# The opening of a two-layer trunk: the norm row cleared and spread by products over 128 partitions, the first half slab's split on VectorE and GpSimd, idle transposes first

## The reference

```
h = rms_norm(x, norm_mix_pre[i])                 # x * rsqrt(mean(x*x) + eps) * w
mix = ssd_mixer(h, ...)  if i == 0 else pool_mixer(h, ...)
x = x + rms_norm(mix, norm_mix_post[i])
f = conv_ffn(rms_norm(x, norm_ffn_pre[i]), ...)
x = x + rms_norm(f, norm_ffn_post[i])
```

## Time and profile before

| | us |
|---|---|
| median of 3 runs | 1150.98 |
| the profiled execution | 1151.16 |
| its span, first to last instruction | 1149.4 |
| TensorE busy | 1141.1 |
| VectorE busy | 684.4 |
| ScalarE busy | 523.9 |
| GpSimd busy | 32.8 |

### The profile page before, as it was taken

How to read it: one execution, slowest core, us unless ns; L and a number is a source line. 1 busy time by engine, 2 the same in 40 slices (tenths; PEclk the granted TensorE clock), 3 DMA queues, 4 the chain that set the end, 5 groups by cost and what they waited for, 6 DMA issues and landing times.

```text
span 1149.4 us, 14668 instructions
## 1 busy us (share of the span) xinstructions
PE 1141.1 (99%) x5734; PEld 956.9 (83%) x5734; DVE 684.4 (60%) x783; ACT 523.9 (46%) x614; POOL 32.8 (3%) x87
## 2 busy tenths in 40 slices
PE   9999999999999999999999999999999999999998
PEld 8888888888788898888888888899888888888886
DVE  5678778888943865565555412487655565562124
ACT  5667676767523644444344211465444344342213
POOL 6000001000000000000000000000000000000000
PEclk9999999999999999999999999999999999999999
DMA  8243444443222323332322332512222323323321
GB/s 271 75 130 129 128 129 129 128 129 129 74 94 90 110 75 117 102 104 80 108 94 88 110 110 92 183 37 74 92 90 93 109 79 103 109 76 111 106 74 74
DMA packets 85246, 121.74 MB, mean 106 GB/s; under 512 B 4167, under 2 KB 71215, under 8 KB 85200
## 3 DMA queue, kind: packets, MB, share of 16 engines
q1 hardware_dynamic: 85018, 121.02, 32.1%
q10 hardware_dynamic: 182, 0.07, 0.0%
HBM read 118.92 MB, written 2.16 MB: 105 GB/s over the span
## 4 chain that ended last, share of the span: by engine, by line
PE 97%; DVE 2%; ACT 0%; issue 0%; POOL 0%; DVEq 0%; POOLq 0%; ACTq 0%
PE bank L994 28%; PE bank L300 18%; PE bank L302 18%; PE bank L301 18%; PE bank L497 6%; PE bank L777 2%; PE bank L786 1%; PE bank L414 1%; PE bank L709 1%; PE bank L736 1%; PE bank L1170 0%; DVE w_lo L270 0%; PE bank L764 0%; PE bank L437 0%; PE bank L432 0%; PE bank L1185 0%
## 5 line engine op out<-in xcount | busy, mean ns | idle before, releaser
L300 PE MATMUL bank<-h_hi,w_hi 128*128 128x512 f32 x928 | 364.1, 392 | 0.0
L302 PE MATMUL bank<-h_hi,w_lo 128*128 128x512 f32 x928 | 361.3, 389 | 0.0
L301 PE MATMUL bank<-h_lo,w_hi 128*128 128x512 f32 x928 | 361.1, 389 | 0.0
L270 DVE TENSOR_TENSOR w_lo<-raw,w_hi 128x2048 fp32r<-128x2048 f32 x90 | 206.2, 2291 | 219.7 <-ACT w_hi L265 219.7
L516 DVE SCALAR_TENSOR_TENSOR tmp<-bank,par,tmp 128x511 f32<-128x511 f32 (+2 forms) x248 | 184.7, 747 | 135.3 <-ACT tmp L507 122.4
L265 ACT ACTIVATE w_hi<-raw 128x2048 fp32r<-128x2048 f32 x90 | 171.5, 1906 | 152.5 <-PE bank L994 152.3
L302 PEld LDWEIGHTS bank<-h_hi,w_lo 128*128 128x128 f32 x928 | 174.2, 188 | 36.6
L301 PEld LDWEIGHTS bank<-h_lo,w_hi 128*128 128x128 f32 x928 | 174.3, 188 | 36.3 <-issue 0.7
L300 PEld LDWEIGHTS bank<-h_hi,w_hi 128*128 128x128 f32 x928 | 174.2, 188 | 36.4 <-issue 0.7
L507 ACT ACTIVATE tmp<-bank,par 128x512 f32<-128x512 f32 x112 | 86.3, 775 | 229.4 <-PE bank L302 209.5
L994 PE MATMUL bank<-w_hi,act_hi 128*128 128x512 f32 x348 | 107.2, 389 | 0.0
(11 more groups left out here) (193 smaller groups left out, 1035.9 us busy)
## 6 DMA issues: line engine op xcount, KB each, us to landing
raw<-in_ffn_w_up SPq DMA_DIRECT2D x44, 1024.0 KB, 5.1
raw<-in_ffn_w_down SPq DMA_DIRECT2D x22, 1024.0 KB, 5.0
raw<-in_ssd_w_in SPq DMA_DIRECT2D x19, 1024.0 KB, 5.5
decay<-ac_dram SPq DMA_DIRECT2D x16, 512.0 KB, 4.3
raw<-in_ssd_w_out SPq DMA_DIRECT2D x8, 1024.0 KB, 4.9
from_start<-ac_dram SPq DMA_DIRECT2D x32, 128.0 KB, 4.0
xres<-in_x SPq DMA_DIRECT2D x4, 512.0 KB, 5.7
result<-xres SPq DMA_DIRECT2D x3, 512.0 KB, 2.6
```

The costliest lines, as they stand in the source:

```text
L270: dve.tensor_tensor(lo[:], raw[n % 2][:], hi[:].bitcast(F32), ALU.subtract).then_inc(lo_ready, 1)
L300: pe.matmul(dst, wh, xh, start=first, stop=False, **kw)
L301: pe.matmul(dst, wh, xl, start=False, stop=False, **kw)
L302: return pe.matmul(dst, wl, xh, start=False, stop=last, **kw)
```

## The change

VectorE first clears all 128 partitions of `pre_b` (new semaphore `pre_clear`), and ScalarE's queue waits for that before it loads the norm row into partition 0. The spread then multiplies the whole 128x128 tile of ones with all 128 partitions of `pre_b`, of which 127 are zero. The high part of the first half slab moves from ScalarE to VectorE, behind the scaling of chunk 1; its low part moves from VectorE to GpSimd, ahead of the window matrices. TensorE starts with nine idle transposes once the identity is there, then waits for the other constants and the norm row; five follow the spread. One parameter piece of 4 KB moves from ScalarE's queue to SP's.

```diff
-        def first_part_hi(act):
-            act.wait_ge(part_in, 16)
-            act.activation(w_hi[0][:, FIRST_PART], raw[0][:, FIRST_PART], ACT.Copy).then_inc(part_hi, 1)
+        def first_part_hi(dve):
+            dve.wait_ge(part_in, 16)
+            dve.tensor_copy(w_hi[0][:, FIRST_PART], raw[0][:, FIRST_PART]).then_inc(part_hi, 1)
...
-        def first_part_lo(dve):
-            dve.wait_ge(part_hi, 1)
-            dve.tensor_tensor(w_lo[0][:, FIRST_PART], raw[0][:, FIRST_PART], w_hi[0][:, FIRST_PART].bitcast(F32),
+        def first_part_lo(pool):
+            pool.wait_ge(part_hi, 1)
+            pool.tensor_tensor(w_lo[0][:, FIRST_PART], raw[0][:, FIRST_PART], w_hi[0][:, FIRST_PART].bitcast(F32),
                               ALU.subtract).then_inc(part_lo, 1)
...
-                pe.matmul(bank[:, PRE_BANK + j, :], ones[0:1, :], pre_b[0:1, j * T:(j + 1) * T], start=True,
+                pe.matmul(bank[:, PRE_BANK + j, :], ones[:], pre_b[:, j * T:(j + 1) * T], start=True,
                           stop=True).then_inc(pre_spread, 1)
...
             first_load(sp, w_in_slabs[Z_SLABS + X_SLABS])
-            load_params(sp, par_pieces[4:])
+            load_params(sp, par_pieces[3:])
...
             pool.wait_ge(consts, 4)
+            first_part_lo(pool)
...
         def _(pe):
+            pe.wait_ge(consts, 3)
+            keep_busy_pe(pe, 9)
             pe.wait_ge(consts, 4)
-            keep_busy_pe(pe, 4)
             spread_pre_pe(pe)
-            keep_busy_pe(pe, 4)
+            keep_busy_pe(pe, 5)
...
         def _(act):
+            act.wait_ge(pre_clear, 1)
             act.dma_start(pre_b[0:1, :], norm_mix_pre[0:1, :]).then_inc(pre_in, 16)
-            load_params(act, par_pieces[:4])
+            load_params(act, par_pieces[:3])
             act.wait_ge(consts, 4)
             root_table_act(act)
             x_stats_act(act, 0, 0)
             x_stats_act(act, 0, 1)
-            first_part_hi(act)
...
         def _(dve):
+            dve.memset(pre_b[:, :], 0.0).then_inc(pre_clear, 1)
             prime(dve, "vector")
...
             scale_dve(dve, 0, 1, pre_view(), (pre_spread, 2))
+            first_part_hi(dve)
             last_part_hi(dve)
             features_dve(dve, 0, 0)
             features_dve(dve, 0, 1)
-            first_part_lo(dve)
             last_part_lo(dve)
```

More of the change, by code:

```diff
@@ L195, in hybrid_trunk @@
         x_sq, x_rms, x_rr, xn_ready = sem("x_sq"), sem("x_rms"), sem("x_rr"), sem("xn_ready")
-        pre_spread, pre_kept, xn_half = sem("pre_spread"), sem("pre_kept"), sem("xn_half")
+        pre_clear, pre_spread, pre_kept, xn_half = sem("pre_clear"), sem("pre_spread"), sem("pre_kept"), sem("xn_half")
         tr_done, h_hi_ready, h_ready = sem("tr_done"), sem("h_hi_ready"), sem("h_ready")
```

## The result

The changed kernel takes 1152.88 us (median of 16 runs, 1152.09 to 1153.75) against 1150.72 us before (16 runs, 1149.89 to 1151.81): ratio 1.0019, 95% interval 1.0012 to 1.0025. It is 2.2 us slower where 1.4 us less was forecast, and outside the range.

What follows compares the result with a forecast made beforehand. TensorE, busy 1141.1 of 1149.4 us, was taken as the bound; pass 2 ending at 15.1 instead of 16.49 saves 1.4 us, giving 1149.6 against the median of 1150.98. Range 1148.8 to 1151.5 us.

Steps and rivals of the forecast that it cites:

- Clearing and the norm row: Opening: memset takes 0.69 us, the row's DMA is issued at about 1.55 and lands at 4.09, upper bound 5.75.
- The spread: Norm row's products on TensorE: lower level for all but the last piece, over at 7.6 us (bounds 5.9 and 7.87).
- The wait that I priced at 0.37 us: TensorE's new idling for the norm row, after nine idle transposes end at 3.72 us.
- VectorE, ScalarE's queue: Opening: table load at 3.3, first reciprocal at 6.44, chunk 1 scaled by 9.86, casts by 11.1, fourth h_lo at 13.65.
- TensorE: Opening: chunk 1's transposes start at 9.9, block products at 11.2, pass 2 ends at 15.1 against 16.49: 1.4 us less.
- GpSimd's low part: First half slab's subtraction: 2.4 us after the second cast at 11.1, done at 13.5, at worst 14.05, hidden.
- (b): Rival: GpSimd gets the port pair before VectorE's second cast; pass 2 ends at 17.45, 1.0 slower, 1152.0 us; chance 0.09.
- (d): Rival: norm row lands at 5.75, spread ends at 9.53, pass 2 at 16.6, 1151.1 us; chance 0.07.
- (c): Rival: TensorE's gaps keep the level low through pass 1; pass 2 ends at 17.8, 1.3 slower, 1152.3 us; chance 0.06.
- (a): Rival: the level rises no earlier than before, near 12.5; pass 2 ends at 16.6, 1151.1 us; chance 0.16.
- The base: Profile of the kernel before: pass 2 ends at 16.49 us, span 1149.4, execution 0.18 above the median of 1150.98.

Runs made afterwards that it cites:

- the second profile: The changed kernel run again without an edit, against the kernel before; its profile ended pass 2 at 18.47 us, against 17.35 in the first.
- row_ahead: Changed kernel with the norm row's DMA at the head of SP's queue, behind the clearing and ahead of all loads: 1150.93 us (one run).
- spread_only: Kernel before with only the clearing, the wait for it and the 128-row spread added: 1152.99 us.
- gap_filled: Changed kernel with 20 idle transposes ahead of the spread instead of nine: median 1150.81 us, against 1150.87 before.
- row96: Changed kernel with the norm row on partition 96, partitions 0 to 95 cleared beside the load, and a 97-row spread: median 1149.87 us.
- row96_only: Kernel before with only the norm row on partition 96, its clearing and the 97-row spread: 1149.55 us, ratio 0.9990.
- row96_split_back: row96 with the half slab split as in the kernel before (high part on ScalarE, low part on VectorE): median 1149.91 us.
- row96_early: row96_only with six idle transposes from the identity on instead of four from the triangle on: 1149.61 us, ratio 0.9989.
- before_again: The kernel before run again without an edit, for its profile: pass 2 ended at 15.80 us, not 16.49.
- split_only: Kernel before with only the moved split (first half's high part on VectorE, low part on GpSimd): 1150.88 against 1150.87 us.
- one_row: Changed kernel without the clearing and with the one-row spread of before: 1.5 us faster than the changed kernel, 0.8 above before.

## Why the prediction was wrong, point by point

**Clearing and the norm row: wrong, and the first step that failed.** I had it issued at 1.55 and landed at 4.09. VectorE began at 1.10 and not at the other engines' 0.81, the memset took 0.92 and not 0.69, so the issue was at 2.04; the flight took 3.70 to 4.87 us in four profiles, not 2.54. The landing at 5.74 is near the upper bound of this very step (5.75, the 4.2 us of a transfer issued into traffic), but by luck: 1.55 + 4.2 there, 2.04 + 3.70 here, and the second profile has 6.91. I had that row and took the other, because it was the same transfer. But in the rows before it was issued together with the first x chunk, and the change put it behind both x chunks; row_ahead shows that without loads ahead of it (and on SP's queue) it lands in 1.73 us at most, clearing and all.

**The spread: wrong, and the second step.** I let the level rise during it. It rose at 10.8, behind it (at about 10.5, at its very end, in the second profile). The wait that I priced at 0.37 us was 1.91 (3.07 in the second profile), and with it nine idle transposes were worth nothing: the kernel with the old four and the late row, spread_only, takes the same time. That this, and not the lateness alone, is the larger part, gap_filled shows: with the row later still (6.27), the medians differ by 2.2 us. The early row has a further part: row96 is 0.75 below its before, gap_filled 0.06.

**VectorE, ScalarE's queue: right in kind.** First root used at 6.82 (6.44 forecast), the table load at 3.93 (3.3 forecast, at most 3.85); the gap between last scaling and h_lo is as worked out (casts of 0.68 and 0.69, h_lo in 2.47). All of it stood 2 us later, behind the spread. The moved parameter piece did nothing visible.

**TensorE: the structure right, the start wrong.** From chunk 1's scaling on, the steps were 1.09, 0.44 and 3.96 us. They began at 11.86 instead of 9.9.

**GpSimd's low part: right, with a risk wrongly weighed.** 2.71 us with the cast ahead of it (2.4 forecast), over by 15.3 and hidden. The port's order (b) went as I said in the changed kernel's profile, and against VectorE in row96's, where its data came late.

**The rivals.** (d), the row at 5.75, is what happened, with 0.07 for its chance. Its spread end (9.53, measured 9.65) and its last h_lo (15.6, measured 15.4) were right; its price of 0.1 us was not, for pass 2 ended 0.86 us later than before. I let h_lo decide, and had left out that transposes, idle transposes and 32 products follow chunk 1's scaling one by one: 11.86 + 1.09 + 0.44 + 3.96 = 17.35. (c), a gap that keeps the level down, was at work at the same time. I had priced and weighed the two as alternatives though the late row makes the gap. (a) falls with gap_filled and row96: idle transposes and wide, mostly zero rows both raise the level.

**The base.** The profile of before was a late draw of its own opening (16.49, again 15.80). Of the 2.2 us between the medians the two first profiles show 0.86 at the end of pass 2; the second pair shows 18.47 - 15.80 = 2.67. The typical difference lies between. What sets the point of the rise from run to run stays open.

## What to carry to other kernels

- A preparation that a DMA must wait for can cost more than its own time where the DMA was among the first to be issued: here 1.23 us of waiting moved the landing by 2.4 to 3.6 us. Prepare what the DMA doesn't write (here, the row on partition 96), and the wait goes: 1149.55 us, 1.0 below before, with no other edit. No version of this study is clearly better.
- Warming work ahead of a wait counts if it goes on until the level has risen: 9 transposes and a gap of 1.91 us gave nothing, 20 and a gap of 0.66 us gave 2.2 us. Where the wait varies, as the row's landing did by 1.2 us, leave room for it.
- When two rivals share a cause, price them together.

## What the runs showed of the hardware that I had not expected

- A 4 KB load took at most 1.73 us with no load ahead of it (row_ahead), 2.54 as the first beside two 512 KB loads on another queue, and 3.70, 3.81, 4.24 and 4.87 when it was issued 1.2 us later than before.
- With a spread of 97 rows, 96 of them zero, the upper level came at 5.8, 7.3, 7.4 and 9.2 us (row96, row96_only, row96_split_back, row96_early); with one-row products at 11.4, 11.8, 12.7 and 13.4 (before_again, split_only, before, one_row).
- A VectorE cast of 0.69 us lasted 2.42 us when GpSimd had begun a subtraction 0.5 us earlier, and ended 0.56 us after it.
- VectorE's first instruction started at 1.10 us, 0.29 later than those of ScalarE's queue, SyncE's and GpSimd.
